# The memory keys and values and half of the normalisation, moved beside the first projection pass of each layer

## The reference, cut to what matters

```python
def rmsnorm(x, g):
    r = lax.rsqrt(jnp.mean(xf * xf, axis=-1, keepdims=True) + EPS)
    return xf * r * g
def mem_kv(mem, g, w):
    kv = rmsnorm(mem, g) @ w                 # (256, 1024) @ (1024, 1024), in both layers
    return kv[..., :X_WIDTH], kv[..., X_WIDTH:]     # keys, values: outputs too
for l in range(DEPTH):                       # y_p (2048, 1024), y_s (32, 1024)
    h_p, h_s = rmsnorm(y_p, norm_pre[l]), rmsnorm(y_s, norm_pre[l])
    mk_p, mv_p = mem_kv(mem_prompt, mem_norm[l], w_mem_kv[l])
    # z = h @ W_in: 5128 columns in layer 0, 3072 in layer 1, split in queries, keys, values, gates, memory queries
    y = y + rmsnorm(gated_out(mix(z), mem_attend(xq, mk, mv), gate, w_out[l]), norm_post[l])
```

## Time and profile before

| | |
|---|---|
| median of the runs | 4075.17 us |
| the profiled execution, its own time | 4075.3 us |
| its span, first to last instruction | 4073.8 us |
| PE busy | 3561.2 us, 87% of the span |
| DVE busy | 1884.2 us, 46% |
| ACT busy | 1320.7 us, 32% |
| POOL busy | 336.6 us, 8% |
| mean granted TensorE clock | 0.935 of full speed |
| DMA, mean | 129 GB/s |

### The profile page before, as it was taken

One profiled execution on the slowest core, in us unless ns is written; L12 is line 12 of the kernel. 1 busy time (PEld: TensorE's weight loads), 2 busy tenths in 40 slices (PEclk: granted clock), 3 DMA queues, 4 the chain that ended last, 5 costly groups with the idle time before them and its releaser, 6 DMA issues. The chain is left out here.

```text
span 4073.8 us, 56573 instructions
## 1 busy us (share of the span) xinstructions
PE 3561.2 (87%) x19825; PEld 3098.8 (76%) x19825; DVE 1884.2 (46%) x3378; ACT 1320.7 (32%) x2438; POOL 336.6 (8%) x549
## 2 busy tenths in 40 slices
PE   5699996799999999878888887899599599996999
PEld 4699996688888887667777776688499577774687
DVE  4311322356666654456666665432311234574432
ACT  1211222245555543445545553111211253310111
POOL 0131000001111110100101000000000000121000
PEclk8799998899999999989999998899799799997899
DMA  4333332567767763322222221432222233565332
GB/s 137 98 98 98 126 95 90 146 199 243 232 216 240 236 201 113 102 82 106 103 83 90 96 86 46 127 116 88 91 95 95 85 124 122 157 215 167 114 108 79
DMA packets 385337, 523.94 MB, mean 129 GB/s; under 512 B 52855, under 2 KB 275064, under 8 KB 380495
## 3 DMA queue, kind: packets, MB, share of 16 engines
q1 hardware_dynamic: 317255, 398.72, 31.3%
q0 software_dynamic: 30624, 93.22, 6.9%
q10 hardware_dynamic: 37248, 29.37, 2.3%
HBM read 388.83 MB, written 132.74 MB: 128 GB/s over the span
## 5 line engine op out<-in xcount | busy, mean ns | idle before, releaser
L382 ACT ACTIVATE z_st_p<-bank 128x352 f32<-128x352 f32 (+3 forms) x325 | 168.1, 518 | 755.3 <-PE bank L365 754.7
L1333 PE MATMUL bank<-w_hi_o,b_hi_o 128*128 128x512 f32 x816 | 328.2, 402 | 70.8 <-DVE w_lo_o L1375 70.8
L338 DVE CAST w_hi_p<-w_raw_p 128x1024 fp32r<-128x1024 f32 (+1 forms) x130 | 89.3, 687 | 538.9 <-PE bank L365 509.1
L365 PE MATMUL bank<-h00hi,w_hi_p 128*128 128x352 f32 x984 | 319.9, 325 | 10.7 <-DVE w_lo_p L340 7.2
L1334 PE MATMUL bank<-w_hi_o,b_lo_o 128*128 128x512 f32 x816 | 324.2, 397 | 0.0
L1335 PE MATMUL bank<-w_lo_o,b_hi_o 128*128 128x512 f32 x816 | 324.1, 397 | 0.0
L365 PE MATMUL bank<-h00hi,w_lo_p 128*128 128x352 f32 x984 | 316.6, 322 | 0.0
L365 PE MATMUL bank<-h00lo,w_hi_p 128*128 128x352 f32 x984 | 316.6, 322 | 0.0
L365 PE MATMUL bank<-h01hi,w_hi_p 128*128 128x512 f32 x656 | 269.2, 410 | 9.0 <-DVE w_lo_p L340 9.0
L365 PE MATMUL bank<-h01lo,w_hi_p 128*128 128x512 f32 x656 | 258.0, 393 | 0.0
L365 PE MATMUL bank<-h01hi,w_lo_p 128*128 128x512 f32 x656 | 257.8, 393 | 0.0
(11 more groups left out here) (361 smaller groups left out, 8697.0 us busy)
## 6 DMA issues: line engine op xcount, KB each, us to landing
z<-z_st_p SPq DMA_DIRECT2D x128, 512.0 KB, 2.8
k_raw_sf<-in_cache_fox_k SPq DMA_DIRECT2D x128, 512.0 KB, 4.2
v_raw_sf<-in_cache_fox_v POOLq DMA_DIRECT2D x128, 512.0 KB, 4.5
w_raw_p<-in_fox_w_in SPq DMA_DIRECT2D x80, 512.0 KB, 5.1
b_raw_o<-bT SPq DMA_DIRECT2D x32, 768.0 KB, 7.4
w_raw_p<-in_pool_w_in SPq DMA_DIRECT2D x48, 512.0 KB, 4.7
out<-tok_fa ACTq DMA_DIRECT2D x64, 256.0 KB, 2.3
w_raw_o<-in_w_out ACTq DMA_DIRECT2D x24, 512.0 KB, 4.0
```

What stands on the lines that cost most here:

```text
L365: last = nc.tensor.matmul(out, wt[:, u, k, :], h[:, k, at0:at0 + width], start=(m == 0), stop=(m == MM - 1))
L382: nc.scalar.activation(z_st[0:rows, t % 2, at0:at0 + width], banks[n % 2][0:rows, 0:width], func).then_inc(z_read, 1)
L1333: nc.tensor.matmul(out, bh, w_hi[:, k, cols], start=(k == 0), stop=False)
```

## The change

`memory_kv` is gone as a stage of its own. Its work for one layer is `memory_rows`, a `Work` of 15 steps; both run beside p00, that of layer 0 between tiles 0.5 and 9, that of layer 1 between 9 and 17. `norm_transpose` stays for the first half (n00, n10). The second half is `norm_rows`, a `Work` of 11 steps, which fills `h01hi`, `h01lo` beside p00 between tiles 28 and 40, and `h11hi`, `h11lo` beside p10 between tiles 0.5 and 23. The sample's memory attention in p00 moves from tiles 18 to 39 to tiles 17.7 to 28, with as many steps. The buffers of the two passes of a layer are now shared, and a barrier over all engines stands between p00 and p01.

```diff
+def pass_buffers(nc, stack, tag):
+    shapes = (("w_raw", [P, 2, KT, P], F32), ("w_hi", [P, 2, KT, P], F32R), ("w_lo", [P, 2, KT, P], F32R), ("z_st", [P, 2, SEQ // 2 + NS], F32))
+    return [stack.enter_context(nc.sbuf_tensor(f"{n}_{tag}", shape, dt)) for n, shape, dt in shapes]
+def project_pass(nc, tag, banks, w, h_hi, h_lo, zT, tiles, chunks, stores, bufs, rows, works, past_gates=None):
...
+def memory_rows(nc, stack, room, tag, const, banks, mem, gain, w, k_out, v_out, plan, freed=()):
...
+    K0 = 5
+    STEPS = K0 + KT + 2
+    def sp(sp):
+        for i in range(STEPS):
+            if i == 0:
+                for sem, v in freed:
+                    sp.wait_ge(sem, v)
                 for t in range(NT):
+                    sp.dma_start(x[:, t, :], mem[t * P:(t + 1) * P, :]).then_inc(x_in, 16)
+                sp.dma_start(g_bc[:, :], gain.partition_broadcast(P)).then_inc(g_in, 16)
+            k = i - K0 + 2
+            if 0 <= k < KT:
+                if k >= 2:
+                    sp.wait_ge(wl_d, k - 1)
+                sp.dma_start(raw[:, k % 2, :], w[k * P:(k + 1) * P, :]).then_inc(w_in[k % 2], 16)
+            if i == K0 + KT:
                 for n in range(2 * NT):
+                    t, half = divmod(n, 2)
+                    sp.wait_ge(ev, n + 1)
+                    sp.dma_start((k_out, v_out)[half][t * P:(t + 1) * P, :], kv[:, half, :]).then_inc(out_d[half], 16)
+            if i == STEPS - 1:
+                for half in range(2):
+                    sp.wait_ge(out_d[half], 16 * NT)
+            yield
+    def act(act):
+        for i in range(STEPS):
+            if i == 1:
+                act.wait_ge(x_in, 16 * NT)
+                for t in range(NT):
+                    if t:
+                        act.wait_ge(sq_d, t)
+                    nc.scalar.activation(xn[:, :], x[:, t, :], ACT.Square, accum_out=ss[:, t:t + 1]).then_inc(sq_d, 1)
+            if i == 2:
+                act.wait_ge(ms_d, 1)
+                nc.scalar.activation(ms[:, :], ms[:, :], ACT.Sqrt).then_inc(rt_d, 1)
+            if 3 <= i < 3 + NT:
+                t = i - 3
+                for j in range(2):
+                    act.wait_ge(tr_d, 2 * t + j + 1)
+                    nc.scalar.copy(mT_hi[:, 4 * j:4 * j + 4, t * P:(t + 1) * P], T_BANKS[j][:, :].rearrange("p (k n) -> p k n", k=4)).then_inc(hi_d, 1)
+            if i == K0 + KT:
+                act.wait_ge(k_d, KT)
+                for n in range(2 * NT):
+                    if n >= 2:
+                        act.wait_ge(out_d[n % 2], 16 * (n // 2))
+                    nc.scalar.copy(kv[:, n % 2, :], O_BANKS[n][:, :]).then_inc(ev, 1)
+            yield
+    def dve(dve):
+        def normed(t):
+            if t:
+                dve.wait_ge(tr_d, 2 * t)
+            nc.vector.scalar_tensor_tensor(xn[:, :], x[:, t, :], ri[:, t:t + 1], g_bc[:, :], ALU.mult, ALU.mult).then_inc(xn_d, 1)
+        for i in range(STEPS):
+            if i == 1:
+                dve.wait_ge(sq_d, NT)
+                nc.vector.tensor_scalar(ms[:, :], ss[:, :], 1.0 / D, EPS, ALU.mult, ALU.add).then_inc(ms_d, 1)
+            if i == 2:
+                dve.wait_ge(rt_d, 1)
+                nc.vector.reciprocal(ri[:, :], ms[:, :]).then_inc(ri_d, 1)
+                dve.wait_ge(ri_d, 1)
+                dve.wait_ge(g_in, 16)
+                normed(0)
+            if 3 <= i < 3 + NT:
+                t = i - 3
+                for j in range(2):
+                    at = (slice(None), slice(4 * j, 4 * j + 4), slice(t * P, (t + 1) * P))
+                    dve.wait_ge(hi_d, 2 * t + j + 1)
+                    nc.vector.tensor_tensor(mT_lo[at], T_BANKS[j][:, :].rearrange("p (k n) -> p k n", k=4), mT_hi[at].bitcast(F32), ALU.subtract).then_inc(lo_d, 1)
+                if t + 1 < NT:
+                    normed(t + 1)
+            k = i - K0 + 1
+            if 0 <= k < KT:
+                dve.wait_ge(w_in[k % 2], 16 * (k // 2 + 1))
+                if k >= 2:
+                    dve.wait_ge(k_d, k - 1)
+                nc.vector.tensor_copy(w_hi[:, k % 2, :], raw[:, k % 2, :]).then_inc(wh_d, 1)
+                dve.wait_ge(wh_d, k + 1)
+                nc.vector.tensor_tensor(w_lo[:, k % 2, :], raw[:, k % 2, :], w_hi[:, k % 2, :].bitcast(F32), ALU.subtract).then_inc(wl_d, 1)
+            yield
+    def pe(pe):
+        for i in range(STEPS):
+            if 3 <= i < 3 + NT:
+                t = i - 3
+                pe.wait_ge(xn_d, t + 1)
+                for j in range(2):
+                    if t:
+                        pe.wait_ge(lo_d, 2 * t - 1 + j)
+                    for k in range(4):
+                        last = nc.tensor.transpose(T_BANKS[j][:, k * P:(k + 1) * P], xn[:, (4 * j + k) * P:(4 * j + k + 1) * P], ident[:, :])
+                    last.then_inc(tr_d, 1)
+            k = i - K0
+            if 0 <= k < KT:
+                if k == 0:
+                    pe.wait_ge(lo_d, 2 * NT)
+                pe.wait_ge(wl_d, k + 1)
+                for n in range(2 * NT):
+                    t, half = divmod(n, 2)
+                    cols = slice(half * XW, (half + 1) * XW)
+                    a_hi, a_lo = mT_hi[:, k, t * P:(t + 1) * P], mT_lo[:, k, t * P:(t + 1) * P]
+                    nc.tensor.matmul(O_BANKS[n][:, :], a_hi, w_hi[:, k % 2, cols], start=(k == 0), stop=False)
+                    nc.tensor.matmul(O_BANKS[n][:, :], a_lo, w_hi[:, k % 2, cols], start=False, stop=False)
+                    last = nc.tensor.matmul(O_BANKS[n][:, :], a_hi, w_lo[:, k % 2, cols], start=False, stop=(k == KT - 1))
+                last.then_inc(k_d, 1)
+            yield
+    return Work(STEPS, plan, dict(sp=sp, pe=pe, act=act, dve=dve)), [(out, 16 * NT) for out in out_d]
...
+def norm_rows(nc, stack, room, tag, const, banks, rows, gain, hT_hi, hT_lo, plan, freed=()):
...
+    LEAD = 2
+    STEPS = LEAD + NT + 1
+    def act(act):
+        for i in range(STEPS):
+            t = tile(i, 0)
+            if t is not None:
+                u = t % 2
+                act.wait_ge(x_in[u], 16 * (t // 2 + 1))
+                if t >= 2:
+                    act.wait_ge(tr_d, 2 * (t - 1))
+                nc.scalar.activation(xn[:, u, :], x[:, u, :], ACT.Square, accum_out=ss[:, u:u + 1]).then_inc(sq_d, 1)
+                act.wait_ge(ms_d, t + 1)
+                nc.scalar.activation(ms[:, u:u + 1], ms[:, u:u + 1], ACT.Sqrt).then_inc(rt_d, 1)
+            t = tile(i, 1)
+            if t is not None:
+                for j in range(2):
+                    act.wait_ge(tr_d, 2 * t + j + 1)
+                    nc.scalar.copy(hT_hi[:, 4 * j:4 * j + 4, t * P:(t + 1) * P],
+                                   banks[2 * (t % 3) + j][:, :].rearrange("p (k n) -> p k n", k=4)).then_inc(hi_d, 1)
+            yield
...
+    def pe(pe):
+        for i in range(STEPS):
+            t = tile(i, 1)
+            if t is not None:
+                pe.wait_ge(xn_d, t + 1)
+                if t >= 3:
+                    pe.wait_ge(lo_d, 2 * (t - 2))
+                for j in range(2):
+                    for k in range(4):
+                        last = nc.tensor.transpose(banks[2 * (t % 3) + j][:, k * P:(k + 1) * P],
+                                                   xn[:, t % 2, (4 * j + k) * P:(4 * j + k + 1) * P], ident[:, :])
+                    last.then_inc(tr_d, 1)
+            yield
+    return Work(STEPS, plan, dict(sp=sp, pe=pe, act=act, dve=dve))
...
-        for l in range(2):
-            memory_kv(nc, f"mk{l}", const, banks, mem_prompt.rearrange("a m d -> (a m) d"), mem_norm[l], w_mem_kv[l], *mems[l])
...
+            rows, bufs = Rows(), pass_buffers(nc, s0, "p0")
-                hi, lo = half_states(0, 0, s1, xp, xs, norm_pre[0])
-
-                def works(stack, landed):
-                    sample, _ = sample_memory(0, stack, stack, z0, 3 * D, 3 * D + XW + D, [(XQ + 2, 0), (len(tiles) - 2, 14)],
-                                              lambda sp: landed(sp, XQ - 1))
-                    return [sample]
-                project_pass(nc, "p00", banks, fox_w_in, hi, lo, z0, tiles, CHUNKS[0], STORES[0], works, (page_table, cache_logf, past))
+                with ExitStack() as sems:
                     with ExitStack() as room:
-                        gates, ends_g = sample_gates(nc, stack, room, const, banks[2:8], z0, F_ROW, fox_b_f, past, fox_lf_s, sufT,
+                        kv0, ends0 = prompt_rows(0, sems, room, [(0.5, 0), (9, 15)])
+                    with ExitStack() as room:
+                        kv1, ends1 = prompt_rows(1, sems, room, [(9, 0), (17, 15)], ends0)
+                    with ExitStack() as room:
+                        sample, ends_s = sample_memory(0, sems, room, z0, 3 * D, 3 * D + XW + D, [(XQ + 1.7, 0), (28, 14)],
+                                                       rows.when(XQ - 1), ends1)
+                    hi1, lo1 = states(0, 1, s1)
+                    hi0, lo0 = states(0, 0, sems)
```

(16 more changed lines are left out.)

182 lines of the change are left out of this document (100 added, 82 removed).

## The result

The changed kernel takes 3940.77 us (median of 4 runs, 3935.28 to 3948.36), beside 4074.42 us for the kernel before in the same job. The ratio is 0.9676, interval [0.9656, 0.9696]: about 132 us faster. The forecast was 3953 us, with a range from 3943 to 3980. So the direction and the mechanism came out as forecast, but the gain is some 10 us larger and the median lies 2 us under the range. The profiled execution is the fastest of the four, 3935.28 us (its span is 3933.8), 5.5 us under the median; that has to be kept in mind when its stages are added up.

A forecast was written before the change was run, and what follows sets the result against it. PE was taken to bound the passes, while the removed stages were chains of waits. 188.9 us removed less 66.6 added gave -122.3, so 4075.3 became 3953 us, with 3943 to 3980 for 8 in 10.

The forecast's parts named there:

- What was removed: The two memory_kv stages, n01 and n11 leave the path: 96.23, 46.20 and 46.47 us, together 188.9 us.
- the table load: In n00, now first to use the root on ACT, loading its table stands on the path: +1.0 us.
- the barrier: Between p00 and p01, a second meeting of the engines costs between 0 and 3.1 us; 1 taken.
- What was added on PE: In p00 and p10, 192 matmuls (43.5 us), 160 transposes (15.8) and broken pace (3.3): 62.6 us, not hidden.
- 36 visits: In p00 and p10, each visit of foreign work breaks PE's pace by 0.09 us: 3.3 us.
- Late copies: ACT copying chunks out too late for PE in the passes: between -3.4 and 47 us, taken as +2.
- The reasoning by position: In p00, a full sample-attention step at a chunk's end makes ACT miss its 7.6 us by 1.5; new steps fit.
- ACT late at every visit: Rival, 14%: in the passes every visit costs PE 1.3 us, 47 instead of 2, so 3998 us.
- The table switches drain: Rival, 4%: ten more table loads in ACT's queue each make PE 1.4 us late, 14 us, so 3967 us.
- The clock falls: Rival, 3%: steps tear holes in p00 and p10, mean clock drops to 0.76, 276 us more, 4229 us.
- PE's share is partly hidden: Rival, 7%: idle ends of p00 and p10 take some work, or clock restarts vanish; 10 us less, 3943 us.
- What follows each seam stays as it was: After the removed stages, n00 still begins with its gain and rows, p01 and p11 with their first weights; no change costed.

The follow-up runs named there:

- e3: Changed kernel with only the memory keys and values beside p00, the second halves' normalisation again separate stages: 4029.13 us, ratio 0.9891 to the kernel before.
- e4: Changed kernel with only the second halves' normalisation beside p00 and p10, memory keys and values again separate stages: 3989.09 us, ratio 0.9789 to the kernel before.
- e5: Changed kernel with p00's sample-attention and normalisation steps all at the last quarter of a chunk: 3949.33 us, ratio 0.9687 to the kernel before.
- e6: Changed kernel with p00's sample-attention and normalisation steps all in the first quarter of a chunk: 3938.61 us, ratio 0.9664 to the kernel before.
- before again: Unchanged copy of the kernel before, run once more: 4076.01 us, ratio 1.0005 to the kernel before.
- e16: Kernel before with two all-engine barriers right ahead of the fox attention's stage: 4075.47 us, one run.

## Why the prediction came out as it did

**What was removed: right.** 96.23 + 46.20 + 46.47 us went. Between matmul starts the start of the program gives -94.9 (forecast -96.2 + 1.0 of the table load), the two seams -46.4 (forecast -46.2 + 1.0 of the barrier) and -47.2 (forecast -46.5). e3 and e4 confirm them apart.

**What was added on PE: right, one term too large.** PE's timeline in p00 after, around twelve matmuls of the memory keys:

```profile
109.77 0.32 PE L378 MATMUL bank<-h00hi,w_lo_p 128*128 128x352 f32 x1
109.93 0.40 PE L914 MATMUL bank<-w_hi_mk,mT_hi_mk 128*128 128x512 f32 x1
...
112.66 0.32 PE L378 MATMUL bank<-h00hi,w_hi_p 128*128 128x352 f32 x1
112.82 0.32 PE L378 MATMUL bank<-h00lo,w_hi_p 128*128 128x352 f32 x1
```

From 109.93 to 112.66 are 2.73 us for 12, 0.2275 each: the pace that was taken. But the matmul before starts 0.16 us ahead and the one behind follows in 0.16: these visits cost nothing of their own. The 0.09 us is paid only behind transposes, as the eight of layer 0's memory rows show:

```profile
95.72 1.03 PE L903 MATMUL bank<-ident_const,xn_mk 128*128 128x128 f32 x8
96.52 0.41 PE L378 MATMUL bank<-h00hi,w_hi_p 128*128 128x352 f32 x1
96.76 0.32 PE L378 MATMUL bank<-h00lo,w_hi_p 128*128 128x352 f32 x1
```

0.80 us for the eight and 0.24 instead of 0.16 behind them. It is so throughout: behind all 16 visits of twelve matmuls the next follows in 0.16 us, behind all 20 visits of transposes, in p00 and p10, in 0.24 or 0.25. So 16 of 36 visits were costed for nothing, 1.4 us.

**Late copies: a little too large.** +2 taken, +0.5 measured, from four waits instead of three. The reasoning by position was right, as e5 and e6 show; e5's forecast of 12 us was too high, 7.3 us came.

**The rivals.** *ACT late at every visit* is out: 3.9 us in p00, nothing in p10. Even with every step at its worst place (e5) p00 grew by 4.7 us and not by 45. *The table switches drain* is out as a cost. PE's only wait in p10 is the one at its start, though ACT's queue loads a table eight times there, four times ahead of a root (second fence, from ACT's groups: count, busy us, mean ns, idle ahead):

```profile
PE bank L378 <- DVE w_lo_p L353: 8.9, 1, 8.9
```

```profile
L966 ACT ACT_TABLE_LOAD x4 | 5.1, 1283 | 0.1
```

One of them on ACT's timeline, with the root behind it:

```profile
2906.17 1.28 ACT L966 ACT_TABLE_LOAD   x1
2907.47 0.20 ACT L966 ACTIVATE ms_n<-ms_n 128x1 f32<-128x1 f32 x1
```

The root starts 0.02 us after the load's end. The Trainium skill (ScalarE: Activation LUTs, "What ACT_TABLE_LOAD costs") puts a drain of about 1.38 us on top of each switch; the rows show the load's 1.28 us and nothing more, so here the measurement decides against the rule. *The clock falls* is out: 0.99 and 0.98 in the two passes. *PE's share is partly hidden* is out too: p00 and p10 grew by 54.9 + 6.3 = 61.2 us, and PE's share, 62.6 less the 1.4 of the visits and with 0.5 of late copies, is 61.7. This rival's time, 3943, was nearest to the result, but for another reason.

**The step that failed** is "What follows each seam stays as it was": the sum put all that the edit does not touch at nothing, and the low end of the range, 3943, held terms of the edited stages only. Beside it, several terms of the sum were mis-sized, each so that the gain came out too small. Since one pair of profiles is not enough for the split, here it is with averages between matmul starts, over the profiles that have the same code in a stretch. Before are the kernel before and its variants, after the changed kernel and its variants; of the runs of one part alone, only p11 counts e3 (before) and e4 (after):

| | average before, us (profiles) | average after, us (profiles) | difference | forecast |
|---|---|---|---|---|
| to p00 | 157.0 (7) | 60.8 (7) | -96.2 | -95.2 |
| seam to p01 | 58.4 (7) | 12.0 (7) | -46.4 | -45.2 |
| seam to p11 | 57.7 (7) | 10.4 (7) | -47.3 | -46.5 |
| p00 and p10 | 789.1 (7) | 851.2 (4 and 5) | +62.1 | +64.6 |
| p01 | 988.8 (7) | 992.0 (7) | +3.2 | 0 |
| p01 to p10 | 1205.7 (3) | 1200.9 (7) | -4.8 | 0 |
| p11 | 447.8 (8) | 444.3 (6) | -3.5 | 0 |
| o1 | 369.3 (7) | 369.1 (7) | -0.2 | 0 |

The touched stretches come to -127.8 us against a forecast of -122.3, the untouched ones to -5.3; the sum, 133 us, is that of the medians. So the miss is half in the one and half in the other.

In the touched half, the two passes give 2.5 us (visits 1.4 and late copies 1.5, which is 0.4 more than needed) and the start and the seams 3.0. The trace on which the sum was built had the shortest start of seven: 155.7 us, where the others have 156.0 to 158.3. And at p01 something behind the seam did change: its first matmul comes 6.1 us after its first transfer, where before it came after 7.3 (6.1 to 6.6 us in the eight profiles without n01 ahead of it, 6.9 to 7.9 in the eight with it).

In the untouched half the fox stage is shorter by 5 to 8 us between the two pairs of profiles, in e4 by 4.5 to 6.4 and in e3 by 1.7 to 3.6. Four kernels in which barriers were added to the kernel before, one of them with other semaphore numbers, have it at 783 us. p11 is shorter by 3.5 us on average (444.3 us, from 441.1 to 446.2, in the six profiles without n11 ahead of it; 447.8, from 446.0 to 450.4, in the eight with it). p01 is longer by 3 us on average (989.2 to 995.6 against 986.9 to 990.3), and why is open. That p11 follows its time at the lower clock is seen within one and the same code: before again has 446.1 us, of which 29 at the lower level, and e16, the same code in this stage, this row (the stretch of p11):

```profile
3253.60:3704.00 450.40, 429.15 (x2044) 351.46 (x2045) 233.03 (x388) 150.36 (x320) 58.92 (x68) 0.95 0.50 153
```

450.4 us, with 41 of them at the lower level. Why one execution has more of that than another is open. The two groups of p11 hardly overlap, but single profiles of one code differ by more than 3.5 us, so its 3.5 us are likely and not shown. Not tried: taking the barrier between p00 and p01 out of the kernel after, to see whether its fox stage goes back to 788 us.

## What to carry over

A stage whose engines wait for each other in turn is worth its whole length when its work goes beside a pass that is bound by PE, less the packed pace of its matmuls: 188.9 us of stages came back as 61 to 62 us of matmuls, and the pace read from rows gave this to 1.4 us. Put each step right behind the copy-out of a chunk; here that alone was worth 3 to 5 us, and spreading work from a crowded pass to the one before it another 11. A blind range needs a term for what the edit does not touch: here -5 to -8 us of 790 in one loop and up to 9 us of 450 in a pass whose clock varies. And the length of a stage is better taken from more than one profile: the start of this program, down to p00, lasted from 155.7 to 158.3 us.

## What was not expected of the hardware

- A visit of another kind of work in a row of matmuls cost PE 0.09 us behind eight transposes of 128 x 128, and nothing behind twelve matmuls of 512 columns.
- A barrier over all engines between two blocks cost 1.0 us (4.11 against 3.1 us from a last store to the next first transfer), and the same barrier a stage ahead of a loop of 788 us went with 5 us less in it.
- With the same instructions p11 took from 441 to 450 us, with 17 to 41 us of it at the lower clock.
